# Half of one branch's attention weights transposed by VectorE in 32x32 blocks and through DRAM instead of by TensorE, in a two-layer hybrid encoder on one Trainium2 core

## The chip, the core and the metric

The kernel runs on one core of a Trainium2 chip (trn2). The metric is the device time of one execution in microseconds (us), lower is better. The inputs are those of `setup_inputs()`; weights are rearranged on the host before the launch and that is not in the time.

## What is computed

The reference is a trunk of two pre-norm residual layers over 512 tokens of width 1024, all in float32. In each layer the normalised input is projected by `w_in`, and the columns feed three token mixers of width 512: A, gated linear attention (4 heads, chunks of 64); B, differential softmax attention (4 heads, two score maps each); C, windowed attention with three dilations (8 heads of 64). Each is gated, projected back to 1024, merged with per-channel sigmoid gates and sent through `w_out`. The change is in mixer C:

```python
for window, dil in DIL_PATTERNS:                      # (128, 1), (512, 4), (2048, 16)
    o_g, lse_g = dilated_window_attention(qc, kc, vc, dil, window // (2 * dil))
    outs.append(o_g); lses.append(lse_g)
wts = jax.nn.softmax(jnp.stack(lses, axis=0), axis=0)
o_c = jnp.einsum('gbhs,gbhsd->bhsd', wts, jnp.stack(outs, axis=0).astype(f32))
y_c = o_c.transpose(0, 2, 1, 3).reshape(B, S, BRANCH_W).astype(x.dtype) * jax.nn.silu(c_g)
```

The three patterns together are one softmax over all 512 keys, with the logarithm of the number of patterns that hold a key (or a large negative number) added to the score. So the kernel needs, for each head of 64 and each block of 128 queries, a 128x512 tile of scores, its softmax, and the product of that with the values.

## The kernel before

**Groups.** A layer is worked in `NG` = 4 groups; group `i` holds head `i` of mixer A, head `i` of mixer B (two score maps) and heads `2i`, `2i+1` of mixer C. So there are 8 groups in all, and the first group of each layer has its own copy of the code (`first` is true), since the layer's norm is still being worked out; the other three run as a loop (`Fori`). After the four groups a layer has a branch stage (24 tiles `z`) and an output stage (8 tiles).

**Projections.** Each product with a weight tile is three float32r matmuls for each of 8 slices of the contraction: high and low parts of the activation (`hh`, `hl`) and of the weight (`wh`, `wl`). One slice is a *step* here, three matmuls of 128x512, and a tile has 8 steps. `product` at L1137 issues them. The two banks `proj` are used in turn; a product begins when the tile two before it has been read out of its bank (`bank_free`). A group's tiles in order are the values (four products of 384 columns, L1241), `a`, `bq`, `bk`, `cq`, `ck`, `ag`, `bg`, and then seven *fillers*: `cg`, `m0` to `m5`, 56 steps. `fill(n)` issues the next n of them. They stand between the attention's matmuls, so that TensorE has work while VectorE and ScalarE do the softmax.

**Weights.** SyncE (SP) loads each raw weight tile (512 KB) into one of 3 slots of `raw_w`, as soon as GpSimd (POOL) has split the one that was there. POOL splits it into `wh` (L424) and `wl` (L433, two halves), in one of 4 slots, as soon as TensorE has finished with the tile that was there. POOL also rotates mixer C's queries and keys (L471 to L475, L357). SP's queue holds, besides, the load of `up` for the next group.

**Attention.** 16 score tiles j = 0 to 15 are made by `scores(p)`, two at a time, into the banks `score0` and `score1`. Tiles 0 to 7 are mixer B's (four query blocks, two maps), 8 to 15 mixer C's. For each, VectorE (DVE) takes the row maximum (`row_max`: L958 for B; L964 for C, which also adds the mask and writes the negated scores to `sneg`), and ScalarE (ACT) the exponential with the row sum (`exp`, L721). 12 *units* u make the weights: units 0 to 3 are B's query blocks, from two tiles each, units 4 to 11 mixer C's, from tile j = u + 4 each. `weights(u)` on DVE takes the reciprocal of the sum (L1003) and scales the tile into `w` (L1005, for B L996 and L998). `turn_weights(u)` on TensorE (PE) transposes the four 128x128 blocks of `w` into a bank `turn` (L1302), and `turned(u)` on ACT copies the bank into `wt` or `wt1` (L729). At last `values` multiplies the transposed weights with the values (L1310): for B into `obank` after unit 3, for C into `mbank` at the end of the group, 16 matmuls of 64 output rows. DVE gates the result into `y` (L1038).

**Order on PE.** It is written out by hand. In numbers of steps: `scores(0)`, 4, `scores(1)`, 5, mixer A's outputs, unit 0, then for units 1 to 3 a pair of scores, 5 steps and the unit, then 3 steps, mixer B's values; then for units 4 to 9

```python
                    for u in range(4, 10):
                        if u % 2 == 0:
                            scores(u // 2 + 3)
                        fill(3 if u in (5, 7) else 4)
                        turn_weights(u)
```

then 4 steps, units 10 and 11, 3 steps and mixer C's values. `scores(p)` waits until the banks it overwrites were read. ACT's order has, besides the exponentials and copies, `tanh_gate` (for `cg`, which DVE then reads out of its bank, L941), `merge_gate(0)` to `merge_gate(5)` (L712: each reads one of `m0` to `m5` out of its bank, with a store to DRAM behind it), and the norms of A and B (L763 to L767, two activation table loads and three activations), after `merge_gate(2)`.

**End of the program.** The last output tile is worked in two halves of the tokens. `last_spread(h)` on PE (L1417) spreads a norm's factor into two banks, one for DVE (L1100) and one for ACT, POOL; both wait for both.

## Time and profile before

| | |
|---|---|
| median of 3 runs | 1237.7 us (1237.18 to 1238.46) |
| the profiled execution | 1239.5 us, of which its span is 1237.7 us |
| PE busy | 1215.9 us, 98% of the span |
| DVE busy | 700.7 us, 57% |
| ACT busy | 440.2 us, 36% |
| POOL busy | 832.3 us, 67% |
| DMA | 148.63 MB, 53136 packets |
| granted TensorE clock, mean | 0.995 |

A busy share is that of the whole span. A matmul's row gives its start and how long it was in the pipeline; the pace is the distance of the starts. PEld is the loading of weights into the array and overlaps PE. An idle time stands in brackets behind the instruction that ended it, with its releaser.

### The profile page before, as it was taken

What the parts mean: (1) busy time and instruction counts of PE and PEld (TensorE: products, weight loads), DVE (VectorE), ACT (ScalarE), POOL (GpSimd) and SP (SyncE); (2) the same over time, 40 slices, a digit from 0 to 9 for tenths busy, and PEclk for the clock granted to TensorE, in tenths of its full rate; (3) what the DMA queues carried; (4) which work ended last, traced back from release to release, by engine and by line L of the source; (5) the groups of instructions that cost most, each with busy time, mean ns of one, the idle gap of its engine ahead of it and who ended that gap; (6) DMA issues with size and microseconds to landing.
All of it is one profiled execution on the core that took longest, in us unless ns stands there. A gap on an engine that the chain in (4) does not pass through costs nothing.

```text
span 1237.7 us, 17755 instructions
## 1 busy us (share of the span) xinstructions
PE 1215.9 (98%) x5892; PEld 991.0 (80%) x5892; DVE 700.7 (57%) x1045; ACT 440.2 (36%) x800; POOL 832.3 (67%) x598
## 2 busy tenths in 40 slices
PE   7999999999999999999999999999999999999997
PEld 5877888788878887787888778887888788777886
DVE  6686227533753385677658841584257335648853
ACT  6425523542454235100253353245314532450011
POOL 5787377738762976677749753985398549857881
PEclk9999999999999999999999999999999999999998
DMA  6333233323332333374244222523252315336612
GB/s 240 102 108 124 96 102 106 111 94 108 104 104 93 119 102 124 126 259 154 90 155 143 87 97 81 159 79 110 73 165 85 120 51 153 102 102 223 218 69 69
DMA packets 53136, 148.63 MB, mean 120 GB/s; under 512 B 6880, under 2 KB 10464, under 8 KB 52704
## 3 DMA queue, kind: packets, MB, share of 16 engines
q1 hardware_dynamic: 30144, 103.04, 24.7%
q10 hardware_dynamic: 22944, 44.98, 11.8%
q8 instruction: 26, 0.43, 0.1%
q14 instruction: 22, 0.18, 0.0%
HBM read 114.45 MB, written 16.78 MB: 106 GB/s over the span
## 4 chain that ended last, share of the span: by engine, by line
PE 92%; DVE 4%; DMA 1%; issue 1%; ACT 1%; ACTq 0%; POOLq 0%; POOL 0%; DVEq 0%
PE proj L1137 52%; PE proj L1241 10%; PE turn L1376 4%; PE turn L1302 3%; PE score L1376 3%; PE score L1294 3%; PE score L1295 2%; PE mbank L1310 2%; PE obank L1310 2%; PE mbank L1376 2%; PE obank L1376 2%; PE proj L1155 1%; PE obank L1329 1%; DMA big<-big 1%; DVE yl L1048 1%
## 5 line engine op out<-in xcount | busy, mean ns | idle before, releaser
L433 POOL TENSOR_TENSOR wl<-raw_w,wh 128x512 fp32r<-128x512 f32 x352 | 505.1, 1455 | 31.7 <-POOL wh L424 31.7
L424 POOL TENSOR_SCALAR wh<-raw_w 128x1024 fp32r<-128x1024 f32 x176 | 213.6, 1214 | 287.3 <-issue 102.4
L1137 PE MATMUL proj<-hh,wh 128*128 128x512 f32 x1016 | 403.4, 397 | 0.5 <-DVE big L1075 0.5
L1137 PE MATMUL proj<-hh,wl 128*128 128x512 f32 x1016 | 398.2, 392 | 0.0
L1137 PE MATMUL proj<-hl,wh 128*128 128x512 f32 x1016 | 397.4, 391 | 0.0
L1137 PEld LDWEIGHTS proj<-hh,wh 128*128 128x128 f32 x1016 | 191.5, 188 | 40.7 <-issue 1.3
L1137 PEld LDWEIGHTS proj<-hh,wl 128*128 128x128 f32 x1016 | 191.1, 188 | 41.2
L1137 PEld LDWEIGHTS proj<-hl,wh 128*128 128x128 f32 x1016 | 191.5, 188 | 38.9
L544 ACT ACTIVATE six<-big 128x512 f32<-128x512 f32 x23 | 14.4, 626 | 198.1 <-DVE big L1075 198.1
L964 DVE CUSTOM_DVE_ANT_0 six<-score,lmask 128x512 f32<-128x512 f32 x64 | 43.2, 683 | 66.4 <-PE score L1295 66.4
L922 DVE TENSOR_TENSOR group<-big,group 128x512 f32<-128x512 f32 x24 | 37.6, 1617 | 71.7 <-ACT big L641 71.4
L729 ACT ACTIVATE big<-turn 128x512 f32<-128x512 f32 x96 | 56.1, 593 | 60.4 <-PE turn L1302 59.7
L721 ACT ACTIVATE six<-score,negmax 128x512 f32<-128x512 f32 x64 | 43.5, 684 | 82.4 <-DVE negmax L958 82.3
L1241 PE MATMUL proj<-wh,hh 128*128 128x384 f32 x192 | 64.9, 338 | 0.0
L1241 PE MATMUL proj<-wh,hl 128*128 128x384 f32 x192 | 64.3, 335 | 0.0
L1241 PE MATMUL proj<-wl,hh 128*128 128x384 f32 x192 | 64.2, 335 | 0.0
L1294 PE MATMUL score<-yh 128*128 128x512 f32 x128 | 57.0, 445 | 4.0 <-DVE group L953 3.8
L357 POOL TENSOR_TENSOR yh<-big,yh 64x1024 fp32r<-64x1024 f32 x16 | 38.4, 2399 | 32.4 <-ACT yh L664 30.9
L721 ACT ACTIVATE six<-six,negmax 128x512 f32<-128x512 f32 x64 | 45.9, 718 | 32.0 <-DVE negmax L964 32.0
L1302 PE MATMUL turn<-ident,w 128*128 128x128 f32 x384 | 56.3, 272 | 0.0
L1302 PEld LDWEIGHTS turn<-ident,w 128*128 128x128 f32 x384 | 46.6, 139 | 10.5
L624 ACT ACTIVATE big<-proj 128x512 f32<-128x512 f32 x32 | 19.2, 599 | 95.4 <-PE proj L1137 95.2
(239 smaller groups left out, 1923.4 us busy)
## 6 DMA issues: line engine op xcount, KB each, us to landing
raw_w<-weights SPq DMA_DIRECT2D x175, 512.0 KB, 3.3
gate_scratch<-gstage ACTq DMA_DIRECT2D x48, 256.0 KB, 2.1
six<-gate_scratch ACTq DMA_DIRECT2D x16, 768.0 KB, 5.1
big<-big ACTq DMA_DIRECT2D x64, 128.0 KB, 3.6
yh<-yh ACTq DMA_DIRECT2D x64, 128.0 KB, 2.4
big<-x_t SPq DMA_DIRECT2D x4, 512.0 KB, 6.4
big<-x_t SPq DMA_DIRECT2D x1, 2048.0 KB, 9.0
x_scratch<-big SPq DMA_DIRECT2D x1, 2048.0 KB, 7.3
```

The source lines that it names most:

```text
L357: return eng.tensor_tensor(yh[other, q_of(n, head):low_of(n, head) + 1:4, :], t[own, 0:2, :], yh[own, q_of(n, head):high_of(n, head) + 1:2 ...
L424: pool.tensor_scalar(wh[:, slot, :, :], src, 1.0, 1.0, ALU.mult, ALU.mult).then_inc(pool_high.sem, 1)
L433: ins = pool.tensor_tensor(wl[:, slot, half, :], src[:, half, :], wh[:, slot, half, :].bitcast(F32), ALU.subtract)
L721: act.activation(probs[:, j % 4, :], src, ACT.Exp, bias=negmax[:, j:j + 1], scale=k, accum_out=sums[:, j:j + 1]).then_inc(exp_done.sem, 1)
L729: act.activation((wt if u < 4 or u % 2 == 0 else wt1)[:, :, q:q + P], turn[u % 2][:, :].rearrange("p (k q) -> p k q", k=QB), ACT.Copy).the ...
L964: dve.tensor_tensor_reduce(sneg[:, j % 2, :], score[j % 2][:, :], lmask[:, S - P - P * b:2 * S - P - P * b], -1.0, 3.0e38, ALU.add, ALU.mi ...
L1137: last = pe.matmul(dst, a[:, slot, k, :], b[:, k, :], start=(k == 0 and a is wh and b is hh), stop=(k == KT - 1 and a is wl))
L1241: last = pe.matmul(proj[b % 2][:, 0:3 * P], a(k)[:, P * b:P * b + P], c[:, 0:3, k, :], start=(k == 0 and n == 0), stop=(k == KT - 1 and n ...
L1294: pe.matmul(score[head][:, :], yh[:, q_of(n, head), q], yh[:, high_of(n, head), :], start=True, stop=False)
L1302: last = pe.transpose(turn[u % 2][:, P * k:P * k + P], w[:, u % 2, P * k:P * k + P], ident[:, :])
L1310: last = pe.matmul(dst, v[:, k, cols], weights[:, k, :], start=(k == 0), stop=(k == QB - 1))
L1376: last = pe.matmul(zbanks[zt % 6][:, :], a[:, SLOT[c % BRANCH_SLOTS], n, :], (yl if is_low else yh)[:, b, :], start=(k == 0 and a is wh an ...
```

## The change

Units 4 to 9 (`VIA`) are no longer transposed by PE. For them:

- DVE only takes the reciprocal (`inverse`); ACT scales the tile in place in `probs` (`scale`); DVE transposes its 32x32 blocks (`turn_32`) into a buffer of two units (`pair_buffer`: `w` for the pairs 4, 5 and 8, 9, and two tiles of `group` for the pair 6, 7).
- SP sends each pair of units to DRAM with four DMAs, one for each 32 partitions, in runs of 256 bytes (`send`), and brings it back with four into `wt1` or `wt`, in runs of 1024 bytes (`bring`). The blocks are put in their places by the DRAM addresses.
- C's values wait for all three pairs (`back`).

Score tile j of mixer C is now query block j % 4 of head (j - 8) // 4, so that a pair is two neighbouring query blocks of one head. The tokens of the pairs come back interleaved by 32, and DVE undoes that as it gates `mbank` into `y`: four instructions of 64x128, two of 64x128 and one of 64x256 in the place of one of 128x512. Units 10 and 11 are scaled in `probs` and transposed by PE from there. The orders on PE, ACT, DVE and SP behind mixer B's values are written out anew: on ACT the norms of A and B stand ahead of `merge_gate(3)` and the last two exponentials. In a layer's first group 3 steps of the fillers stand ahead of `scores(0)` and 3 fewer at the end. At the end of the program `last_spread` signals each of its two banks by itself.

```diff
+VIA = list(range(4,10))
+BY_PE = [u for u in range(12) if u not in VIA]
+PAIRS = len(VIA) // 2
...
+        def by_quarter(t, n):
+
+            return t.rearrange("p n s -> p (n s)").rearrange("p (c k n j) -> p k c n j", c=4, k=QB, n=2)[:, :, :, n, :]
+
+        def pair_buffer(m):
+
+            return group[:, 8:10, :] if m == 1 else w
...
+        def w_free(G, u):
+
+            if u in VIA:
+                m = VIA.index(u) // 2
+                return sent[m - 2].at(G, 64) if m >= 2 else turn_done.at(G, len([n for n in BY_PE if n < u]))
+            return turn_done.at(G, BY_PE.index(u - 2) + 1)
...
+            def send(G, m):
+
+                sp.wait_ge(*turned_32.at(G, 2 * m + 2))
+                for a in range(4):
+                    sp.dma_start(turned_d[m, :, :, a, :], pair_buffer(m)[32 * a:32 * a + 32, :, :].rearrange("i n s -> i (n s)").rearrange(
+                        "i (x j) -> i x j", j=64)).then_inc(sent[m].sem, 16)
+
+            def bring(G, m):
+
+                u = VIA[2 * m]
+                if u == 4:
+                    sp.wait_ge(*c_parts.at(G, 1))
+                    apart(sp)
+                sp.wait_ge(*sent[m].at(G, 64))
+                if u == 8:
+                    sp.wait_ge(*out_done.at(G, 3))
+                    apart(sp)
+                k, q = (0 if u < 8 else QB), 2 * P * (u % 4 // 2)
+                for c in range(4):
+                    sp.dma_start(big[32 * c:32 * c + 32, k:k + QB, q:q + 2 * P], turned_d[m, :, QB * c:QB * c + QB, :, :].rearrange(
+                        "i x a j -> i x (a j)")).then_inc(back.sem, 16)
...
                         unit(L, i * GU + (4 + j), arrival(4 + j)[0])
+                        if j == 15:
+                            send(L * NG + i, 0)
+                    send(L * NG + i, 1)
+                    bring(L * NG + i, 0)
+                    send(L * NG + i, 2)
+                    bring(L * NG + i, 1)
+                    bring(L * NG + i, 2)
...
+                    def scale(u):
+
+                        j = 2 * u if u < 4 else u + 4
+                        act.wait_ge(*rs_ready.at(G, VIA.index(u) + 1))
+                        act.activation(probs[:, j % 4, :], probs[:, j % 4, :], ACT.Copy, scale=rs[:, j:j + 1]).then_inc(scaled.sem, 1)
...
-                act.wait_ge(*spread.at(h, 1))
+                act.wait_ge(*spread.at(h, 2))
...
+                    def inverse(u):
...
+                            j = u + 4
+                            dve.wait_ge(*exp_done.at(G, j + 1))
+                            dve.reciprocal(rs[:, j:j + 1], sums[:, j:j + 1]).then_inc(rs_ready.sem, 1)
+
+                    def turn_32(u):
+                        j = 2 * u if u < 4 else u + 4
+                        dve.wait_ge(*scaled.at(G, VIA.index(u) + 1))
...
+                        if u >= 2:
+                            dve.wait_ge(*w_free(G, u))
+                        dve.transpose(by_quarter(pair_buffer(VIA.index(u) // 2)[:, :, :], u % 2), probs[:, j % 4, :].rearrange("p (k c j) -> p k c j", k=QB, c=4)).then_inc(turned_32.sem, 1)
...
-                    dve.scalar_tensor_tensor(y[:, 2 * NG + i, :], mbank[:, :], 0.5, sg[:, 2, :], ALU.mult, ALU.mult).then_inc(y_read.sem, 1)
+                    h0, h1 = rows_of(0), rows_of(1)
+                    for b in range(QB):
+                        dve.scalar_tensor_tensor(tokens(y[h0, 2 * NG + i, :], b), by_token(mbank[h0, :], b), 0.5, tokens(sg[h0, 2, :], b), ALU.mult, ALU.mult)
+                    for b in range(2):
+                        dve.scalar_tensor_tensor(tokens(y[h1, 2 * NG + i, :], b), by_token(mbank[h1, :], b), 0.5, tokens(sg[h1, 2, :], b), ALU.mult, ALU.mult)
+                    t = slice(2 * P, 4 * P)
+                    dve.scalar_tensor_tensor(y[h1, 2 * NG + i, t], mbank[h1, t], 0.5, sg[h1, 2, t], ALU.mult, ALU.mult).then_inc(y_read.sem, 1)
...
+                    if first:
+                        fill(3)
                     scores(0)
...
+                    scores(5)
+                    fill(6)
+                    pe.wait_ge(*y_read.at(G, 2))
+                    mean_of(obank, 2)
+                    scores(6)
                     fill(4)
+                    scores(7)
+                    fill(13)
                     turn_weights(10)
+                    fill(2)
                     turn_weights(11)
-                    fill(3)
+                    fill(1 if first else 4)
                     assert filled == KT * len(FILLERS)
                     pe.wait_ge(*r_done.at(G, 1))
-                    values(12, out_done, (mbank[0:HD, :], slice(2 * P, 2 * P + HD), wt),
-                           (mbank[HD:P, :], slice(2 * P + HD, 3 * P), wt1))
+                    pe.wait_ge(*back.at(G, PAIRS * 64))
+                    pe.wait_ge(*wt_ready.at(G, len(BY_PE)))
+                    values(out_done, (mbank[0:HD, :], slice(2 * P, 2 * P + HD), wt1),
+                           (mbank[HD:P, :], slice(2 * P + HD, 3 * P), wt))
...
-                last.then_inc(spread.sem, 1)
+                    last.then_inc(spread.sem, 1)
```

**On DVE**, from the first row maximum of mixer C that follows mixer B's weights to the units that PE still transposes, before (ISA rows are the row maxima of L964, RECIPROCAL and TENSOR_SCALAR the weights):

```order
L1003 RECIPROCAL rs<-sums 128x1 [waits exp_done,turn_done]
L1005 TENSOR_SCALAR w<-six,rs 128x512 [waits dve_grp]
L964 ISA six,negmax<-score,lmask 128x512 [waits score_done,exp_done]
L964 ISA negmax 128x1
L1026 TENSOR_TENSOR yl<-group,yl 128x512 [waits sq_high_done,sq_done]
L1027 SCALAR_TENSOR_TENSOR y<-obank,sc,group 128x512
```

and with the change, to the third pair:

```order
L1098 RECIPROCAL rs<-sums 128x1 [waits exp_done] x2
L1045 ISA six,negmax<-score,lmask 128x512 [waits score_done,exp_done]
L1045 ISA negmax 128x1
L1110 STREAM_TRANSPOSE w<-six 128x4x4x32 [waits sent0,scaled]
L1045 ISA six,negmax<-score,lmask 128x512 [waits score_done,exp_done]
L1045 ISA negmax 128x1
L1110 STREAM_TRANSPOSE w<-six 128x4x4x32 [waits sent0,scaled]
L1151 TENSOR_TENSOR y<-y,group 128x512 [waits y_read,r_done]
L1152 TENSOR_TENSOR y<-y,group 128x512
L1084 RECIPROCAL rs<-sums 128x1 [waits exp_done]
L1086 TENSOR_SCALAR six<-six,rs 128x512 [waits dve_grp]
```

A unit of `VIA` is a reciprocal and a transpose on DVE now, with ACT's scaling between them; the last two transposes stand behind the row maxima of the last two tiles, and wait for the first pair's store (`sent0`).

**On SP**, from the last but one weight load of a group to the end of the group's body:

```order
L413 DMA raw_w<-weights 128x1024
L420 DMA turn_scratch<-w 512x1x64 [waits turned_32]
L420 DMA turn_scratch<-w 512x1x64 x3
L413 ISA [waits split_done]
L413 DMA raw_w<-weights 128x1024
L420 DMA turn_scratch<-group 512x1x64 [waits turned_32]
L420 DMA turn_scratch<-group 512x1x64 x3
L435 DMA big<-turn_scratch 32x4x256 [waits sent0]
L435 DMA big<-turn_scratch 32x4x256 x3
L420 DMA turn_scratch<-w 512x1x64 [waits turned_32]
L420 DMA turn_scratch<-w 512x1x64 x3
L435 DMA big<-turn_scratch 32x4x256 [waits sent1]
```

The last of a group's weight loads, and the loads of the next group behind them, now stand behind waits for DVE's transposes and for stores.

## Rows read from the trace of the kernel before

**Rows 1.** The page: busy time, granted clock and the chain that ended last.
```profile
PE 1215.9 (98%) x5892; PEld 991.0 (80%) x5892; DVE 700.7 (57%) x1045; ACT 440.2 (36%) x800; POOL 832.3 (67%) x598
...
PE 92%; DVE 4%; DMA 1%; issue 1%; ACT 1%; ACTq 0%; POOLq 0%; POOL 0%; DVEq 0%
```
**Rows 2.** Timeline of PE (start us, us), third group: turns and what stands around them.
```profile
356.48 0.39 PE L1295 MATMUL score<-yh 128*128 128x512 f32 x1
...
373.23 0.60 PE L1302 MATMUL turn<-ident,w 128*128 128x128 f32 x4
...
376.44 0.60 PE L1302 MATMUL turn<-ident,w 128*128 128x128 f32 x4
...
382.69 3.65 PE L1310 MATMUL mbank<-big,group 128*64 128x512 f32 x16
```
**Rows 3.** Timeline of PE, second group: first and last of 16 products, one slot each.
```profile
199.66 0.39 PE L1137 MATMUL proj<-hh,wl 128*128 128x512 f32 x1
...
203.29 0.39 PE L1294 MATMUL score<-yh 128*128 128x512 f32 x1
```
**Rows 4.** Timeline of PE, first groups of both layers: around the first scores.
```profile
82.59 0.47 PE L1294 MATMUL score<-yh 128*128 128x512 f32 x1 [1.98 <-DVE group L953]
...
94.70 0.40 PE L1137 MATMUL proj<-hh,wh 128*128 128x512 f32 x1
...
685.76 0.47 PE L1294 MATMUL score<-yh 128*128 128x512 f32 x1 [1.87 <-DVE group L953]
```
**Rows 5.** A window in layer 1's first group: busy times by engine, then granted clock.
```profile
684.00:692.00 8.00, 6.24 (x20) 5.00 (x21) 6.62 (x14) 2.08 (x5) 7.64 (x5) 0.79 0.00 0
```
**Rows 6.** Timeline of DVE: gate of `cg`; scalings and row maximum of mixer C.
```profile
98.18 0.67 DVE L941 SCALAR_TENSOR_TENSOR group<-group,proj 128x512 f32<-128x512 f32 x1
...
350.22 1.30 DVE L1005 TENSOR_SCALAR w<-six,rs 128x512 f32<-128x512 f32 x1
...
356.64 0.69 DVE L964 CUSTOM_DVE_ANT_0 six<-score,lmask 128x512 f32<-128x512 f32 x1 [5.12 <-PE score L1295]
...
358.96 0.49 DVE L1005 TENSOR_SCALAR w<-six,rs 128x512 f32<-128x512 f32 x1
```
**Rows 7.** Groups of DVE's instructions: count, busy us, mean ns.
```profile
L1038 DVE SCALAR_TENSOR_TENSOR y<-mbank,group 128x512 f32 x6 | 4.2, 692 | 52.6 <-PE mbank L1310 52.6
L982 DVE SCALAR_TENSOR_TENSOR state<-state,decay,turn 64x128 f32<-64x128 f32 x24 | 8.5, 353 | 0.3
```
**Rows 8.** Timeline of ACT, third group: an exponential, a merge gate, the norms.
```profile
357.37 0.73 ACT L721 ACTIVATE six<-six,negmax 128x512 f32<-128x512 f32 x1 [0.30 <-DVE negmax L964]
...
363.13 0.59 ACT L712 ACTIVATE gstage<-proj 128x512 f32<-128x512 f32 x1
364.26 1.28 ACT L763 ACT_TABLE_LOAD   x1 [0.54 <-ACT gstage L712]
...
368.13 1.06 ACT L767 ACTIVATE group<-group 128x1024 f32<-128x1024 f32 x1
```
**Rows 9.** Timeline of POOL, third group: the split of the last value tile.
```profile
376.11 1.04 POOL L424 TENSOR_SCALAR wh<-raw_w 128x1024 fp32r<-128x1024 f32 x1 [3.38 <-PE proj L1137]
```
**Rows 10.** DMA: share of 16 engines, 1231 to 1237.7 us; then issues, KB each, median us to landing.
```profile
q1 hardware_dynamic: 1383, 1.30, 57.3%
...
raw_w<-weights SPq DMA_DIRECT2D x175, 512.0 KB, 3.3
gate_scratch<-gstage ACTq DMA_DIRECT2D x48, 256.0 KB, 2.1
...
out_t<-y SPq DMA_DIRECT2D x4, 128.0 KB, 2.5
```
**Rows 11.** Timeline, end of layer 0's groups: DVE's low parts, PE's first low products.
```profile
508.03 6.11 DVE L1048 TENSOR_TENSOR yl<-y,yh 128x512 fp32r<-128x512 f32 x10 [0.21 <-DVE y L1038]
...
510.74 2.75 PE L1376 MATMUL score<-yl,wh 128*128 128x512 f32 x8
```
**Rows 12.** Timeline, end of the program: the spread of the first half's factor.
```profile
1225.83 0.61 PE L1417 MATMUL score<-ident,rcol 128*128 128x128 f32 x4
```

163 lines of the change are left out of this document (102 added, 61 removed).

## The prediction

> **What bounds the kernel now.** I read the page first. PE is busy for 98% of the span and carries 92% of the chain that ended last [rows 1]. So an instruction taken from PE is worth its slot, as long as nothing makes PE wait in its place; a busy share of 57% on DVE, 36% on ACT and 67% on POOL says that they have room on average, not that they are on time. Then I read PE's timeline. 16 products start in 3.63 us, 199.66 to 203.29 [rows 3]: one each 0.227 us, a step of three 0.68. Between the turns at 373.23 and 376.44 lie 3.21 us for one turn and 12 products [rows 2]; the products take 2.72, so a unit's turn costs 0.49 us, the slower start behind it included. PE waits inside the groups only twice, ahead of the first scores of each layer's first group, 1.98 and 1.87 us [rows 4]. The windows show what followed the second: over the 8 us from 684 on TensorE was granted 0.79 of its full clock on average [rows 5], that is 3.4 us at its lower level, 1.2 in the place of 2.4 GHz, which cost 1.7 us of matmul time. Behind the first wait, of about the same length, it kept the full level.
>
> **What goes.** 6 turns in each of 8 groups at 0.49: 48 x 0.49 = -23.4 us. ACT copied each of them out of its bank and now scales each tile instead, which is the same work; DVE's scaling becomes a transpose.
>
> **The first groups' fill.** 3 steps (2.04 us) ahead of the first scores fill the waits of 1.98 and 1.87 us [rows 4]: -3.85. But 3 steps more are done at every later place, and a product must find its bank read. `m1` is step 16. Before, it began three steps into the fill behind unit 1; now it begins behind the fourth step of the one behind unit 0. That fill starts at 94.70 [rows 4], four steps later it is 97.4, and `m1` takes the bank of `cg`, which DVE reads from 98.18 for 0.67 us [rows 6]: free at about 98.9. PE waits 1.5 us, in both first groups: +3.0. `m5` comes later, below.
>
> **A group behind mixer B's values.** I lay the new order over the third group's trace. The last matmul of `scores(5)` starts at 356.48 [rows 2], so PE goes on at 356.7: 6 steps to 360.8; the mean's two matmuls to 361.3; `scores(6)`, four slots, to 362.2; 4 steps, 364.9; `scores(7)`, 365.8; 13 steps, 374.7; unit 10, 2 steps, unit 11, 4 steps: C's values could start at 379.8, against 382.69 before [rows 2].
>
> DVE and ACT: a row maximum takes 0.69 [rows 6], an exponential 0.73 and 0.18 more for its sum [rows 8]. ACT's scaling has no row; a merge gate's activation of the same 128x512 takes 0.59 [rows 8], so 0.6. The transpose has no row either. Its bounds are the two durations of the scaling that it replaces, 0.49 alone and 1.30 when a POOL instruction ran at the same time [rows 6]; I take 0.65, nearest to the row maxima, which like it are one pass over a 128x512 tile. The Trainium skill ("SBUF — State Buffer", Who interferes with whom) says that a DVE instruction with at most one SBUF input outside the two-port modes doesn't contend with GpSimd. By that the transposes stay near the low end while POOL splits weights; were they held up as the scalings are, each would be at the upper one.
>
> With these, tile 10's maximum ends at 357.3, the transpose of unit 4 (behind ACT's squares) at 358.5, tile 11's maximum at 360.9, in time for `scores(6)` at 361.3. Maxima 12 and 13 end at 363.3, transposes 6 and 7 at 365.5; ACT ends scaling 9 at 366.9; the maxima of 14 and 15, with transposes 8 and 9 between and behind them, end at 368.7. ACT then does the norms, 4.9 us from table load to end [rows 8], to 371.9, `merge_gate(3)` to 372.5 and its store's issue to 372.9, exponential 14 to 373.8. DVE scales unit 10 from 374.0. There POOL is at work: the split of the last value tile starts when `m4` is done, at 376.11 before [rows 9], at 373.4 now. So the scaling takes up to 1.3 and not 0.49, and PE, there at 374.7, waits about 0.4 us: +0.4 in each of the 6 other groups, +2.4 (bounds 0 and 0.9 each). In a first group `m5` (step 48) is due at 371.3 by the same count, but its bank is `m3`'s, read by `merge_gate(3)` at 372.5: +1.1 in each, +2.2, and the wait at unit 10 is hidden.
>
> **The way through DRAM.** 1383 packets took 57.3% of 16 engines in 6.7 us [rows 10]: 44 ns each, nearly all of 1024 bytes. For a packet of 256 bytes I have no row: not above 44, and, at a quarter of the bytes, not below 11. I take 16 ns, nearer to the low end, since stores of twice the bytes, 256 KB and 128 KB, land in about the same time [rows 10] and so little of it goes by packets. A pair is 2048 packets, 128 on each engine: 2.0 us (1.4 to 5.6) beside the issues of four DMAs, and another 2.1 us, a store's time to land [rows 10], behind the last issue at the most. The third pair starts at 368.9, when SP has the two transposes, and has landed by 373. The way back is 512 packets of 1 KB, 1.4 us of data beside four issues, and 2.5 for 128 KB to land [rows 10]: by 377. C's values are ready to start at 380.1. That hides it with 3 us to spare, 2 in a first group. Cost 0. The first pair's store (361.5 to 365.5) frees `w` for transpose 8 at 366.7, also in time.
>
> SP's queue: the last value tile's load stands behind the first pair, which goes out at 361.5, and is wanted at 373.4; it takes 3.3 us [rows 10]. The next group's `up` and `a` go out behind the third pair's return, at about 375; `up` is wanted at 382, `a`'s split after 380. Nothing there.
>
> **The gate of `mbank`.** One instruction of 0.69 us becomes seven. 64x128 with two tensors takes 0.35 [rows 7]; six at 0.3 and one of 64x256 at 0.4 are 2.2: 1.5 us more. Inside a layer it is covered by the next group's first value product, 4 us. At a layer's end it is not: DVE's low parts start at 508.03, right behind the gate, and PE's 8 products with them take 2.75 us where 1.8 is their pace [rows 11]. PE already waits for DVE there, so the 1.5 us come through, in both layers: +3.0 (bounds +2.3 and +3.8, with the seven at 0.25 to 0.35 and 0.35 to 0.5).
>
> **The end.** DVE no longer waits for the second bank of the spread, which PE starts at 1225.83 [rows 12] and gives away nearly 0.4 us later; the last update follows on it: -0.35. In the second half POOL and ACT still wait for both.
>
> **Sum.** -23.4 - 3.85 + 3.0 + 2.4 + 2.2 + 3.0 - 0.35 = -17.0. The clock's fall in layer 1 I leave in: the wait before it goes, one of 1.5 us comes a little later. The profiled execution took 1239.5 us, its span is 1237.7, and so is the median of the runs: profiled I expect 1222.5, as a median **1220.7**.
>
> **Rivals.** *The added waits don't come* (DVE and ACT a little quicker than I laid them out): -23.4 - 3.85 + 3.0 - 0.35 and 1.7 less for 3.4 us at half clock: 1211.4. For it: every one of these waits is under 1.6 us. Against: a bank's reader is in a fixed order, and `cg`'s gate has its row. Chance 0.10.
>
> *The softmax chain is late.* Transposes at their upper bound, 1.30, put 3.9 us more on DVE by unit 10, of which about 2 reach PE in each group, since exponential 14 waits behind the norms anyway: 8 x 2 = 16 us back, 1236. At half of that, 1229. For it: the two ways from exponential to scaling to transpose cross between ACT and DVE at each unit. Chance 0.24 for 1226 to 1237.
>
> *The third pair is late, and the kernel slower.* Place: PE's last wait of a group, for `back`. All pairs go through one queue. With p ns for a packet of 256 bytes, the second pair's data starts at 365.6 and takes 0.128 p; the first pair's return, 1.4, and the third pair's data, 0.128 p, stand behind it; 1.2 to land and 3.6 for the return: 371.8 + 0.256 p. At 16 ns my time stands; at 32 ns it is 380.0, just in time; at 40 ns 382.1, 2 us late in 8 groups, and the gain is gone; at 44 ns, the row's price for 1 KB, 383.1: 3 us, +24, and if the clock falls behind each such wait as in rows 5, 1.7 more each, +13.6: 1245 to 1258. The Trainium skill ("DMA: Bandwidth & Descriptors", Specifications) says that transfers under 512 bytes make the engine read, modify and write. As a mechanism here that is a packet at twice its time or more, 32 ns and up; it would be at the edge of my slack or past it. No row shows such stores. Chance 0.12 for slower, and 0.04 more that it ends within 0.2%.
>
> *The orders don't do what they say*, for instance a weight load late behind SP's waits, so that POOL and PE start a group late: the slack is 7 us there, so I give it no chance of its own.
>
> **Numbers.** My forecast, 1215 to 1226, has 0.50; the rivals as above. The range leaves out the slow end and the lower half of the first rival: 1213 to 1236. Faster by over 0.2% (which is about what a measurement of this kernel can tell from no change, 2.5 us) 0.84, within it 0.04, slower 0.12.
>
> **What would show it.** PE's turns 192 in the place of 384; no wait ahead of the first scores; waits of PE at L1261 (a filler for its bank) of 1.5 and 1.1 us in two groups; one of about 0.4 at unit 10; none at C's values. Transposes near 0.65 us. The low products at a layer's end over 3.5 us. A wait at the values' line in all 8 groups, with DMA as releaser, would make this wrong, and so would transposes of over 1.2 us.

## The result, and the profile after

| | before | changed |
|---|---|---|
| median | 1238.1 us (4 runs, 1237.2 to 1239.0) | 1262.7 us (4 runs, 1261.7 to 1265.2) |
| ratio | | 1.0205, 95% interval 1.0193 to 1.0217 |
| profiled execution, span | 1239.5, 1237.7 us | 1262.2, 1260.1 us |
| mean granted clock | 0.995 | 0.986 |

The change makes the kernel 2% slower. The forecast, 1220.7, was on the wrong side; the rival that ended on this side (the third pair late, 1245 to 1258) named the place, and even its upper end is 5 us short.

The page of the changed kernel, to be held against [rows 1]: PE is busy for 6.4 us less, but has lost its hold on the chain, in which SyncE's queue and the DMAs now stand.

```profile
PE 1209.5 (96%) x5700; PEld 973.2 (77%) x5700; DVE 708.7 (56%) x1093; ACT 445.5 (35%) x800; POOL 830.7 (66%) x598
...
PE 81%; SPq 7%; DMA 4%; DVE 4%; issue 2%; ACT 1%; DVEq 0%; POOLq 0%; POOL 0%; ACTq 0%
```

PE's waits (engine, line, waited for: us in total, times, longest us):

```profile
PE mbank L1435 <- DMA big<-turn_scratch: 27.0, 8, 3.9
...
PE proj L1261 <- DVE group L1022: 2.8, 2, 1.4
PE proj L1261 <- ACT gstage L782: 2.2, 2, 1.1
PE turn L1428 <- DVE six L1086: 1.8, 8, 0.2
```

The first line is new and is 27 us: C's values (L1435) wait for the pairs in all 8 groups. The next three are the waits that I had priced. The waits ahead of the first scores [rows 4] are gone.

The third group on PE, where [rows 2] shows what stood there before, and then two windows (us, PE, PEld, DVE, ACT, POOL busy, granted clock, DMA share, GB/s):

```profile
389.03 6.63 PE L1435 MATMUL mbank<-big,group 128*64 128x512 f32 x16 [3.49 <-DMA big<-turn_scratch]
```
```profile
384.00:388.00 4.00, 1.54 (x7) 0.94 (x5) 0.00 (x0) 0.60 (x1) 0.00 (x0) 1.00 1.03 255
388.00:396.00 8.00, 6.97 (x18) 2.17 (x19) 0.15 (x1) 0.31 (x1) 3.53 (x3) 0.57 0.58 221
```

The values take 6.63 us where they took 3.65: after the wait of 3.49 us the clock was 0.57 of full on average over 8 us, which is 6.9 us at its lower level, 3.4 us lost. That is the worst of the eight groups: in the other seven, behind waits of 2.85 to 3.87 us, the values take 5.1 to 5.4 us. Over the whole execution the mean of 0.986 is 35 us at that level.

SyncE's queue in the same group, a row for each run of DMA issues:

```profile
366.50 3.37 SPq L420 DMA_DIRECT2D turn_scratch<-w  x4
370.14 0.44 SPq L413 DMA_DIRECT2D raw_w<-weights  x1
370.81 2.93 SPq L420 DMA_DIRECT2D turn_scratch<-group  x4
373.95 2.73 SPq L435 DMA_DIRECT2D big<-turn_scratch  x4
376.80 3.40 SPq L420 DMA_DIRECT2D turn_scratch<-w  x4
380.24 4.64 SPq L435 DMA_DIRECT2D big<-turn_scratch  x8
```

and the end of the chain of waits there, single issues:

```profile
373.95 1.30 SPq L435
...
378.76 1.44 SPq L420
...
384.43 4.48 DMA big<-turn_scratch
```

SyncE issues 20 DMAs from 370.81 on without a pause. Most take 0.43 (loads) or 0.6 us (stores), some 0.8 to 1.4. The third pair's transposes end at 374.1,

```profile
373.41 0.70 DVE L1110 STREAM_TRANSPOSE w<-six 128x512 f32<-128x512 f32 x1
```

but its stores begin at 376.80, behind the first pair's loads; the last load is issued at 384.4 and lands 4.5 us later (a landing is counted from the start of its issue). One of the third pair's transposes had itself waited, for the first pair's store to free `w`:

```profile
372.19 0.71 DVE L1110 STREAM_TRANSPOSE w<-six 128x512 f32<-128x512 f32 x1 [0.43 <-DMA turn_scratch<-w]
```

For landings of stores SyncE itself waits once, for 0.7 us in the whole execution:

```profile
SPq L431 <- DMA turn_scratch<-w: 0.7, 1, 0.7
```

All the while the DMA engines are close to full, where they had been half empty before (here 372 to 376 us of the changed kernel, then of the kernel before):

```profile
372.00:376.00 4.00, 4.00 (x19) 3.34 (x18) 1.93 (x4) 3.95 (x5) 2.35 (x3) 1.00 0.90 245
```
```profile
372.00:376.00 4.00, 4.00 (x22) 3.26 (x21) 3.62 (x10) 2.29 (x6) 0.73 (x1) 1.00 0.59 197
```

### The profile page after: what moved, and what is told of

Read it like the earlier page. It is cut to its first block, busy times and chain, and to the rows that moved or that the text cites. A ratio compares the mean times of both kernels' runs of the same rounds, so it can differ in the third digit from the quotient of the medians.

```text
span 1260.1 us, 17507 instructions
## 1 busy us (share of the span) xinstructions
PE 1209.5 (96%) x5700; PEld 973.2 (77%) x5700; DVE 708.7 (56%) x1093; ACT 445.5 (35%) x800; POOL 830.7 (66%) x598
## 4 chain that ended last, share of the span: by engine, by line
PE 81%; SPq 7%; DMA 4%; DVE 4%; issue 2%; ACT 1%; DVEq 0%; POOLq 0%; POOL 0%; ACTq 0%
PE proj L1261 44%; PE proj L1365 9%; PE turn L1506 4%; SPq L420 3%; PE mbank L1435 3%; SPq L435 3%; PE score L1506 3%; DMA big<-turn_scratch 3%; PE obank L1435 2%; PE score L1418 2%; PE score L1419 2%; PE mbank L1506 2%; PE obank L1506 2%; DMA turn_scratch<-w 1%; PE proj L1279 1%
## 5 line engine op out<-in xcount | busy, mean ns | idle before, releaser
L1435 PE MATMUL mbank<-big,group 128*64 128x512 f32 x128 | 43.3, 839 | 27.0 <-DMA big<-turn_scratch 27.0
L1158 DVE SCALAR_TENSOR_TENSOR y<-mbank,group 64x128 f32 (+1 forms) x32 | 7.1, 276 | 99.9 <-PE mbank L1435 99.9
L1435 PEld LDWEIGHTS mbank<-big,group 128*64 128x64 f32 x128 | 12.7, 191 | 53.7 <-issue 53.7
```

The costliest lines, as they stand in the source:

```text
L1435: last = pe.matmul(dst, v[:, k, cols], weights[:, k, :], start=(k == 0), stop=(k == QB - 1))
```

## The experiments

All times are medians; the ratio is to the kernel before, run on the same chip. "Start of values" is the time from the start of `scores(5)` to that of C's values in the third group (changed kernel: 360.52 and 389.03). It and the waits are those of the profiled execution, which is not the median one: 1243.7 us in run 4, 1265.0 in run 9 and 1234.8 in run 12.

| | median us | ratio, 95% interval | PE's waits at values, us | start of values |
|---|---|---|---|---|
| changed kernel | 1262.7 | 1.0205 (1.0193 to 1.0217) | 27.0 | 28.5 |
| 1 no way back | 1221.4 | 0.9857 (0.984 to 0.9873) | none | 25.0 |
| 2 stores first | 1260.4 | 1.0182 (1.0161 to 1.0204) | 23.1 | 27.6 |
| 3 PE kept busy | 1248.2 | 1.0084 (1.0062 to 1.0106) | 3.1 | 28.2 |
| 4 short runs back | 1240.7 | 1.0009 (0.9996 to 1.0021) | 15.8 | 26.2 |
| 5 heads apart | 1248.3 | 1.0076 (1.0061 to 1.0091) | 5.7 and more | 26.3 |
| 6 all three mends | 1237.5 | 0.9997 (0.9987 to 1.0008) | none | 25.0 |
| 7 two pairs | 1222.9 | 0.9872 (0.9858 to 0.9887) | none | 25.4 |
| 8 gates not stored | 1246.3 | 1.0068 (1.0044 to 1.0093) | 21.8 | 26.0 |
| 9 few bytes | 1259.3 | 1.0154 (1.0138 to 1.017) | 28.2 | 28.2 |
| 10 two pairs, 2 steps ahead | **1219.3** | 0.9845 (0.9832 to 0.9859) | none | |
| 11 two pairs, 0 steps ahead | 1223.3 | 0.9873 (0.9858 to 0.9888) | none | |
| 12 second queue | 1239.3 | 1.0006 (0.9989 to 1.0022) | 12.4 | 25.6 |

### 1. Without the way back

```diff
                     send(L * NG + i, 1)
-                    bring(L * NG + i, 0)
                     send(L * NG + i, 2)
-                    bring(L * NG + i, 1)
-                    bring(L * NG + i, 2)
...
-                    pe.wait_ge(*back.at(G, PAIRS * 64))
+                    for m in range(PAIRS):
+                        pe.wait_ge(*sent[m].at(G, 64))
```

> The changed kernel with the four loads of each pair left out; TensorE waits for the three pairs' stores instead, so the products of units 4 to 9 with the values work on what the buffer held before, and the output is not the reference's. Theory A (the way through DRAM is the whole miss: SyncE issues 24 DMAs a group one behind the other, so the third pair comes late, and each wait is followed by 3.4 us at half clock): the stores have landed at about 383.5 of the third group, TensorE is ready at 385.5, so the wait at the values goes and the falls of the clock with it: 1262.7 - 27 - 15 = about 1221, 1218 to 1225. Theory B (the rest of the sum is off as well: transposes and scalings, or the short stores disturbing other work): over 1228.

1221.4. Everything but the way through DRAM came out as the sum had it, to 0.7 us. The values' row of the third group has no wait and its old 3.65 us:

```profile
376.28 3.65 PE L1432 MATMUL mbank<-big,group 128*64 128x512 f32 x16
```

So the whole miss, 41 us, is at one wait.

### 2. Stores ahead of loads

```diff
                     send(L * NG + i, 1)
-                    bring(L * NG + i, 0)
                     send(L * NG + i, 2)
+                    bring(L * NG + i, 0)
```

> Only the order on SyncE's queue is changed: the second and the third pair's stores go out ahead of all loads. Same DMAs, same bytes. Theory A (order and issue time on SyncE's queue): the third pair's first store is issued when its transposes are there, at about 374.1 in the third group where it was 376.8; the last load lands at about 387.3 instead of 389.0, TensorE is ready at 385.5 and waits 1.8 instead of 3.5 us: 8 x 1.7 = 13 us less, 1249, and 1236 if the clock's falls go with it. Theory B (the data itself, stores of 256-byte packets, fills the time): no change, 1260 to 1265.

1260.4, 2 us less, hardly clear of the scatter, and not 13 to 26. The third pair's stores do start earlier, as expected; but the loads then stand in one block, and end only 1.1 us earlier than in the changed kernel, counted from `scores(5)` (359.55 here):

```profile
373.18 3.09 SPq L420 DMA_DIRECT2D turn_scratch<-w  x4
376.48 6.37 SPq L435 DMA_DIRECT2D big<-turn_scratch  x12
```

My theory that the order on the queue is the fault falls. An order can't shorten 20 issues in a row.

### 3. TensorE kept busy in the wait

```diff
                     pe.wait_ge(*r_done.at(G, 1))
+                    pe.wait_ge(*wt_ready.at(G, len(BY_PE)))
+                    for _ in range(12):
+                        pe.matmul(turn[0][:, :], mean[:, :], hh[:, 0, :], start=True, stop=True)
                     pe.wait_ge(*back.at(G, PAIRS * 64))
```

> Twelve matmuls of 128x512 without use are put on TensorE between its last filler of a group and its wait for the pairs, 2.7 us of work inside a wait of 3.4; nothing else changes. Theory C (of the miss of 42 us some 14 are the clock, which falls behind each idle wait): with a wait of under 1 us the falls go, 1262.7 - 14 = about 1249. If the falls have another cause: 1262, not under 1260. If the matmuls outlast the wait in the first groups, some 1 to 3 us are added in both cases.

1248.2: 14.5 us come back though the pairs are as late as before. The rows: work, a wait of 0.40, the values at their full pace, and full clock behind them.

```profile
382.94 2.97 PE L1485 MATMUL turn<-hh,mean 128*128 128x512 f32 x12
386.31 3.65 PE L1435 MATMUL mbank<-big,group 128*64 128x512 f32 x16 [0.40 <-DMA big<-turn_scratch]
```
```profile
386.00:394.00 8.00, 7.69 (x40) 5.17 (x41) 2.02 (x8) 0.31 (x1) 3.58 (x3) 1.00 0.57 215
```

With a mean clock of 0.997 against 0.986, 28 us fewer at half speed, 14 us by the clock alone. So the 41 us are 27.0 of waiting and 14 of what the clock does behind it.

### 4. Runs of 1024 bytes out and 256 back

```diff
-                    sp.dma_start(turned_d[m, :, :, a, :], pair_buffer(m)[32 * a:32 * a + 32, ...
-                        "i (x j) -> i x j", j=64))
+                    sp.dma_start(turned_d[m, a, :, :, :].rearrange("c i x -> i c x"), pair_buffer(m)[32 * a:32 * a + 32, ...
+                        "i (c x) -> i c x", c=4))
...
-                    sp.dma_start(big[32 * c:32 * c + 32, k:k + QB, q:q + 2 * P], turned_d[m, :, QB * c:QB * c + QB, :, :] ...
+                    sp.dma_start(big[:, k:k + QB, q + 64 * c:q + 64 * c + 64], turned_d[m, c, :, :, :] ...
...
-    turn_scratch = nc.dram_tensor("turn_scratch", (PAIRS, 32, 16, 4, 64), F32, kind="Internal").ap()
+    turn_scratch = nc.dram_tensor("turn_scratch", (PAIRS, 4, 4, 32, 4 * 64), F32, kind="Internal").ap()
```

> The DRAM buffer is laid out so that the stores go in runs of 1024 bytes and the loads in runs of 256; the number of DMAs, their order and bytes stay. Theory A (issue and landing, not packets, set the time): within 3 us of 1262.7. Theory B (a store of 256 bytes costs the engine a second pass, a load doesn't): the last landing comes 1 us or more earlier, 8 us or more faster, under 1255.

1240.7: 22 us less for the same bytes in the same number of packets and DMAs. It isn't the packets' time: a packet of 256 bytes took 19 ns on average in the changed kernel and 18 here, and the time of the pairs' packets in that group, as a share of 16 engines, is about equal (13.1 and 12.7 us). What became shorter is the stores' issue and their landing. Issues of the changed kernel, then of this one (KB each, median us from issue to landing):

```profile
big<-turn_scratch SPq DMA_DIRECT2D x96, 128.0 KB, 3.3
...
turn_scratch<-w SPq DMA_DIRECT2D x64, 128.0 KB, 3.7
turn_scratch<-group SPq DMA_DIRECT2D x32, 128.0 KB, 3.9
```
```profile
big<-turn_scratch SPq DMA_DIRECT2D x96, 128.0 KB, 3.2
...
turn_scratch<-w SPq DMA_DIRECT2D x64, 128.0 KB, 2.7
turn_scratch<-group SPq DMA_DIRECT2D x32, 128.0 KB, 3.0
```

Stores in long runs land 0.9 to 1.0 us sooner; loads in short runs no later. The issue of a store takes 0.44 us where it was 0.64, that of a load 0.63 where it was 0.43 (medians). Which of the two did it this run can't tell. SyncE can issue the third pair's loads when it is through with the second pair's and the third pair's stores have landed. Counted from the start of `scores(5)` in the third group, the one ends at 22.3 and the other at 22.1 us in the changed kernel, at 20.3 and 19.8 here: two ways of nearly the same length, and both became shorter. The last load is issued 1.5 us earlier (22.4 for 23.9) and lands 3.65 us behind its issue where it was 4.48. That DVE no longer waits for the first pair's store gains nothing: the third pair's transposes end at 13.1 for 13.6, but its stores begin at 15.2 and 16.3, when the queue comes to them.

Between the profiled executions, 18.5 us apart, 11.2 are waits. The rest is the clock, 0.991 for 0.986, some 6.5 us: it did not fall behind each wait any more. Two of the eight groups:

```profile
746.95 6.27 PE L1434 MATMUL mbank<-big,group 128*64 128x512 f32 x16 [3.83 <-DMA big<-turn_scratch]
869.80 3.65 PE L1434 MATMUL mbank<-big,group 128*64 128x512 f32 x16 [1.84 <-DMA big<-turn_scratch]
```

### 5. The two heads' products apart

```diff
-                        for k in range(QB):
-                            for dst, cols, weights in products:
+                        for dst, cols, weights in products:
+                            if dst is products[-1][0] and len(products) == 2:
+                                pe.wait_ge(*back[1].at(G, 64))
+                                pe.wait_ge(*wt_ready.at(G, len(BY_PE)))
+                            for k in range(QB):
...
-                    pe.wait_ge(*back.at(G, PAIRS * 64))
+                    pe.wait_ge(*back[0].at(G, 128))
```

> The products with the values are done head by head, not alternating: the first head's eight wait only for the first two pairs, the second head's eight for the third. Nothing else changes. In the third group TensorE is ready at 385.5 and the last load lands at 388.9; the second pair's loads land some 2 us before. So the first head's 1.8 us of products stand inside the wait: 8 x 1.8 = 14 us less, 1248, and down to 1236 if a wait of about 1 us isn't followed by the clock's fall. If the first two pairs come hardly earlier than the third (all DMAs served side by side), no more than 4 us: 1258 to 1262.

1248.3, the number expected, but not by the way expected. The values start 2.2 us earlier than in the changed kernel, with the first head, and the wait is short enough that the clock stays at 1.00 behind it. But the products themselves became slower, as run 6 shows without any wait: 1.8 us in each group. 27.0 - 5.7 - 8 x 0.8 (the second head's wait: this kernel's row takes 6.20 and that of run 6 5.42) = 15 of waiting and 14 of clock are gained, 8 x 1.8 = 14 given back: 1248.

### 6. Short runs back, stores first and heads apart, together

```diff
                     send(L * NG + i, 1)
-                    bring(L * NG + i, 0)
                     send(L * NG + i, 2)
+                    bring(L * NG + i, 0)
...
-                            for dst, cols, weights in products:
+                        for dst, cols, weights in products:
```

on the runs of experiment 4.

> Runs of 1024 bytes out and 256 back, the third pair's stores ahead of the loads, and the heads' products apart. By the run with short runs back, where TensorE was ready at 381.2 and the last load landed at 382.2 of the third group: the first head is in time, the second head's products start at 383.0 and find it there. No wait at the values, no clock fall: 1221, 1219 to 1225, below both kernels. If the stores put first delay the first head's loads past 381.2: 1225 to 1235.

1237.5, the kernel before within its uncertainty, where I expected 1221. There is indeed no wait, and the clock is 0.997. What is left is in the values' row, and in the loads of their weights, inside each block one every 0.43 us (where the blocks meet, two or three, as in the last line):

```profile
379.68 5.42 PE L1437 MATMUL mbank<-big,group 128*64 128x512 f32 x16
380.16 0.14 PEld L1437 LDWEIGHTS mbank<-big,group 128*64 128x64 f32 x1 [0.29 <-issue]
380.59 0.14 PEld L1437 LDWEIGHTS mbank<-big,group 128*64 128x64 f32 x1 [0.29 <-issue]
...
381.44 0.19 PEld L1437 LDWEIGHTS mbank<-big,group 128*64 128x64 f32 x3 [0.29 <-issue]
```

In run 1, where the heads alternate, two of them stand in the same time:

```profile
376.76 0.14 PEld L1432 LDWEIGHTS mbank<-big,group 128*64 128x64 f32 x2 [0.28 <-issue]
377.19 0.14 PEld L1432 LDWEIGHTS mbank<-big,group 128*64 128x64 f32 x2 [0.28 <-issue]
```

5.42 - 3.65 = 1.77 us in 8 groups is 14.2: 1221.4 + 14.2 = 1235.6; the profiled execution took 1236.1.

### 7. Two pairs only

```diff
-VIA = list(range(4,10))
+VIA = list(range(4,8))
...
-                    fill(13)
+                    fill(7)
+                    turn_weights(8)
+                    fill(2)
+                    turn_weights(9)
+                    fill(4)
                     turn_weights(10)
```

Units 8 and 9 get `weights` on DVE and `turned` on ACT again, and DVE's gate of `mbank` is five instructions.

> Only units 4 to 7 go through DRAM, in two pairs; units 8 and 9 are scaled by VectorE and turned by TensorE again. 16 DMAs a group on SyncE's queue in the place of 24. 1220.7 from my own sum, plus 16 turns of 0.49 us = 1228.5, if two pairs are in time (in the third group they would be back at about 381, TensorE comes at 386): 1226 to 1232. If two pairs are late as well: over 1238.

1222.9, better than both kernels and 5.6 under my sum. The loads are issued by 368.3 and there is nothing to wait for:

```profile
363.42 4.89 SPq L435 DMA_DIRECT2D big<-turn_scratch  x8
```
```profile
375.50 3.65 PE L1429 MATMUL mbank<-big,group 128*64 128x512 f32 x16
```

The waits at unit 10 (1.8 us) and for `m3`'s bank (2.2) are gone too, since PE comes to both later; that is 4 of the 5.6.

### 8. The gates' stores left out

```diff
-                        act.dma_start(gate_d[i * 6 + m, :, :], gstage[:, m % 2, :])
+                        if first and L == 0:
+                            act.dma_start(gate_d.rearrange("(g n) p s -> n p g s", n=6)[m], gstage[:, m % 2:m % 2 + 1, :].to_broadcast([P, NG, S]))
+                        else:
+                            act.dma_start(gate_d[i * 6 + m, :, 0:4], gstage[:, m % 2, 0:4])
```

> Beside the three pairs, ScalarE's queue sends the merge gates of 256 KB to DRAM, three of them in that stretch. Here the very first group writes all four groups' gates once and the others store 4 columns instead of 512, so the output is not the reference's. SyncE's queue is as it was. If the DMA engines' own time is what makes the pairs late (they are busy for 0.8 to 1.0 from 368 to 388 of the third group, the three gate stores 2.9 us of it): the last load lands 1.5 to 3 us earlier, 12 to 24 us less and the clock's falls with it, 1225 to 1245. If it is SyncE's issuing alone: no change, 1259 to 1265.

1246.3, just above the range for the engines' own time. SyncE's queue has the same DMAs in the same order, and yet the values start 2.5 us earlier in the third group: the last load is issued 1.4 us earlier and lands in 3.4 us for 4.5. In the first group, which stores four times as much, the wait grew from 2.85 to 12.3 us:

```profile
151.47 6.60 PE L1438 MATMUL mbank<-big,group 128*64 128x512 f32 x16 [12.30 <-DMA big<-turn_scratch]
```

The other seven wait 9.5 us together, 1.4 each for 3.4. Other transfers on the engines, even from another engine's queue, move this wait both ways.

### 9. A sixteenth of the bytes

```diff
-                        "i (x j) -> i x j", j=64)).then_inc(sent[m].sem, 16)
+                        "i (x j) -> i x j", j=64)[:, :, 0:4]).then_inc(sent[m].sem, 16)
...
-                    sp.dma_start(big[32 * c:32 * c + 32, k:k + QB, q:q + 2 * P], ...
+                    sp.dma_start(big[32 * c:32 * c + 32, k:k + QB, q:q + 16], ...
...
-    turn_scratch = nc.dram_tensor("turn_scratch", (PAIRS, 32, 16, 4, 64), F32, kind="Internal").ap()
+    turn_scratch = nc.dram_tensor("turn_scratch", (PAIRS, 32, 16, 4, 4), F32, kind="Internal").ap()
```

> The changed kernel with the same 24 DMAs a group in the same order and with the same number of pieces, but pieces of 16 bytes out (256 before) and 64 back (1024 before), so one sixteenth of the data; most of what is multiplied with the values is what the buffer held, and the output is not the reference's. If the time on the DMA engines holds the pairs up and SyncE's issuing only backs up behind it: the wait at the values goes, 1221 (1219 to 1225), and the issues take 0.43 to 0.64 us with none over 1. If issuing itself is the limit (by its pieces, not its bytes): 20 issues still take 12 us or more from the second pair's transposes, the last load lands less than 1.5 us earlier than in the changed kernel, 1240 to 1263.

1259.3. The numbers are those of the second expectation (20 issues in 16 us, the last load landed 0.4 us earlier), but not for its reason. The DMA engines were only a third to two thirds busy, and no issue on that group's chain took over 1.11 us; but the wait stayed at 28.2 us. SyncE now stood still for landings of stores, in all 8 groups, and the chain shows them:

```profile
SPq L431 <- DMA turn_scratch<-w: 24.4, 8, 4.2
```
```profile
367.11 6.14 DMA turn_scratch<-w
...
373.26 1.11 SPq L435
...
377.90 5.73 DMA turn_scratch<-w
```

A store of 8 KB in pieces of 16 bytes lands 6 us behind its issue, longer than 128 KB in pieces of 256 did. A packet of 16 bytes took 9 ns, so this isn't the packets' time on the engines. The median from issue to landing over the kernel goes with the size of the pieces: 2.7 and 3.0 us at 1024 bytes (run 4), 3.7 and 3.9 at 256, 4.6 and 5.8 here.

```profile
turn_scratch<-w SPq DMA_DIRECT2D x64, 8.0 KB, 4.6
turn_scratch<-group SPq DMA_DIRECT2D x32, 8.0 KB, 5.8
```

As a test of issuing against bytes the run was badly chosen: it took bytes away and lengthened the landing.

### 10 and 11. Two or no steps ahead of the first scores

```diff
                     if first:
-                        fill(3)
+                        fill(2)
                     scores(0)
...
-                    fill(1 if first else 4)
+                    fill(2 if first else 4)
```

> Two pairs through DRAM, and 2 steps instead of 3 ahead of a layer's first scores, 1 more at that group's end. The first step of m1 then stands behind the next pair of scores, where cg's bank has been read: its wait of 1.4 us goes in both layers (-2.8); ahead of the first scores 0.68 us less is covered, of which 0.6 and 0.5 come back as waits (+1.1). 1222.9 - 1.7 = 1221.2. If the bank's wait only moves: 1223 to 1224.

> Two pairs through DRAM, and the 3 steps ahead of a layer's first scores put back to the group's end, as in the kernel before. By my terms: the waits of 1.98 and 1.87 return (+3.85), those for cg's bank go (-2.8), and the clock's fall in layer 1 may return (+1.7): 1222.9 + 1.1 to 2.8 = 1224.0 to 1225.7. If the fill ahead brought nothing: 1222.9 within 0.5.

1219.3 with 2 steps and 1223.3 with none, beside 1222.9 with 3. Run 10 is 1.9 us better than expected: the 1.1 us of waits that I had coming back ahead of the first scores did not come (no wait over 0.2 us is left there). Filling 3 steps ahead brought nothing that can be measured: the waits of 1.4 us for `cg`'s bank cost what the fill gains. With 2 steps neither wait is left; PE's waits over 0.5 us in run 10 are all outside the groups. Without the fill 1.9 us of waiting are back ahead of the first scores in the first layer (full clock behind it, 1.00 from 82 to 90 us). In the second layer there is none at that place, but there are two a little later, 0.71 at unit 0 and 0.99 at a pair of scores. With these 3.6 for my 3.85, and 2.8 off for `cg`'s bank, it would be 1223.7; the other 0.4 is within the runs' scatter (1222.5 to 1225.2).

```profile
82.01 0.47 PE L1412 MATMUL score<-yh 128*128 128x512 f32 x1 [1.90 <-DVE group L1032]
```

### 12. The third pair's loads from ScalarE's queue

On top of run 4, with the stores first:

```diff
                     exp(15)
+                    act.wait_ge(*sent[2].at(G, 64))
+                    for c in range(4):
+                        act.dma_start(big[:, QB:2 * QB, 64 * c:64 * c + 64], turned_d[2, c, :, :, :]...).then_inc(back.sem, 16)
                     turned(10)
```

> Three pairs, runs of 1024 bytes out and 256 back, all stores ahead of the loads on SyncE's queue, and the third pair's four loads issued from ScalarE's queue, behind the last exponential. TensorE is ready for the values 25.0 us after it begins scores(5); with the short runs back the loads were there 26.1 after it. If SyncE's one queue is the limit: the third pair's store has landed at 17.6, ScalarE is free at 19.3 and issues until 21.8, landed at 25.3: waits of 0.3 us, 1221.4 + 2.4 = about 1224 (1221 to 1228). If the landing of the loads grows by what the second queue brings forward: 1236 to 1241, as with the short runs back.

1239.3, as the second expectation had it: no better than run 4, whose interval it shares. The last issue begins 20.1 us behind the start of `scores(5)` (352.75 here), 2.3 earlier than in run 4; but the last load takes 5.30 us to land, where it took 3.65, with the DMA engines full (second row below). The Trainium skill ("DMA: Bandwidth & Descriptors", Rules for kernel authors) says that DMAs spread over more issuing engines gain no bandwidth, since all run on the same 16, and save only the time of issuing. With 2.3 us saved at issuing the trace agrees; that the landing takes 1.7 us longer stands in this trace, not in the rule.

```profile
372.88 5.30 DMA big<-turn_scratch
```
```profile
372.00:376.00 4.00, 3.77 (x21) 2.96 (x20) 1.90 (x3) 1.77 (x4) 2.90 (x3) 1.00 1.25 246
```

## Why the prediction was wrong

Run 1 says that every term of the sum but one held: 1221.4 for 1220.7. (The sum's first term, 48 x 0.49, is 23.5 and not 23.4.) The step that failed is "The third pair starts at 368.9 ... has landed by 373 ... by 377 ... That hides it with 3 us to spare ... Cost 0". Counted from the start of `scores(5)` (355.38 in the trace that I had laid it over; 356.48 is its last matmul), I had the third pair's stores start at 13.5 us, the last load back at 21.6 and PE ready at 24.7. Measured: 16.3, 28.4 and 25.0. The 6.8 us by which the way is longer are

- 0.1: the third pair's transposes end at 13.6, nearly as counted. Within that, "frees `w` for transpose 8 ..., also in time" failed as well: the first pair's store landed at 11.6 and not 10.1, and the transpose waited 0.43 us for it;
- 2.7: its stores then stand in SyncE's queue behind the first pair's four loads. I had priced each pair's way as if it were alone, and looked at the queue only for what stands behind the pairs;
- 2.0: from the first of these stores to the last load's issue 7.6 us for 5.6. An issue takes 0.43 or 0.6 us and more when the engines are full; 12 of them follow one another here;
- 2.0: the last load lands in 4.5 us, not 2.5. I had taken 2.5 from `out_t` [rows 10], four DMAs at the end of the program, where no other queue sends data.

3.1 of it were to spare and PE came 0.3 later than counted: 3.4, for the 3.49 of the trace. The clock did the rest, as the rival had foreseen from [rows 5]; I had it at 1.7 us a group and it averages 1.8.

**The price of a packet** was not the fault: 19 ns for my 16, against 11 to 44. The rival's sum (3 us late at 44 ns) came to the right wait by a wrong cause. The Trainium skill ("DMA: Bandwidth & Descriptors", Specifications) says that transfers under 512 bytes make the engine read, modify and write. The packets' time on the engines shows no doubling: medians of 18 ns for 256 bytes, 28 for 516 and 46 for 1024 in the changed kernel. But the landing of the stores, 3.8 against 2.9 us, and 5 us for 16 bytes, does show that short pieces cost in a store to DRAM and not in a load from it. Whether that is the rule's mechanism no run here can tell. The same page of the Trainium skill (Anatomy of one DMA, on DMAs that GpSimd issues) puts most of a DMA's fixed time, about 2 us, on the wait until the last byte is confirmed in the target memory, longest for DRAM. The stores here are issued by SyncE, and those of run 9, of 8 KB, took 4.6 to 5.8 us with hardly any time on the engines; what that time is made of no run shows.

**What of the lateness is issuing, engine time or landing** isn't one of them alone. In the changed kernel the queue and the landing of the third pair's stores let the third pair's loads go at nearly the same time (22.3 and 22.1 us in the third group), so that shortening one of them alone could gain little there. Runs 2 and 12 changed the issuing (1.1 and, against run 4, 2.3 us earlier) and got 0.9 and 0.6 at the values. Run 8 took transfers off the engines and got 2.5. Run 4 changed the pieces, and with them issues and landings, and got 2.3. My first theory, SyncE's issuing, explains 20 issues in a row but not run 12. Open is how much of the landing at 256 bytes is the pieces' own and how much the full engines': in run 8 the same stores land in 3.0 and 3.3 us where it was 3.7 and 3.9. What is settled is that no order tried brought three pairs back within 25 us, and that two fit (run 7). Run 4's pieces with the stores first, and the heads still alternating, were not tried on one queue.

The other terms, by their rows:

| term | predicted | measured |
|---|---|---|
| `m1` waits for `cg`'s bank | 1.5 us twice | 1.4 twice |
| `m5` waits for `m3`'s bank | 1.1 twice | 1.1 twice |
| unit 10 | 0.4 in 6 groups | 0.2 in 8 |
| first scores | no wait left | none left |
| transpose, scaling | 0.65, 0.6 us | 0.71, 0.72 us |
| `mbank`'s gate | 1.5 us more | 1.1 more: 1.80 for 0.69 |
| low products at a layer's end | 1.5 us more | 1.1 more |
| the end | 0.35 less | DVE's first update starts 0.45 sooner behind the spread |

The gate and the products behind it in run 1, for [rows 11]:

```profile
498.36 0.88 DVE L1155 SCALAR_TENSOR_TENSOR y<-mbank,group 64x128 f32 x4 [7.60 <-PE mbank L1432]
499.25 0.50 DVE L1157 SCALAR_TENSOR_TENSOR y<-mbank,group 64x128 f32 x2
499.67 0.42 DVE L1159 SCALAR_TENSOR_TENSOR y<-mbank,group 64x256 f32 x1
```
```profile
501.96 3.81 PE L1504 MATMUL score<-yl,wh 128*128 128x512 f32 x8
```

All 48 transposes took 704 to 714 ns, though half of them stand beside one of POOL's splits, where scalings had been held up to 1.30 us [rows 6]. The Trainium skill ("SBUF — State Buffer", Who interferes with whom) says that a DVE instruction with at most one SBUF input, outside the two-port modes, doesn't contend with GpSimd; the trace agrees.

## What to carry to other kernels

Work that is taken off the bottleneck and sent through DRAM must be priced as a queue: all its DMAs in order, each with its issue, on engines shared with everything else in that stretch, and with a landing time read from a busy stretch, not from a quiet one. Here the last third of the work was worth 1.5 us at best (1221.4 against 1222.9, and the intervals of the two overlap) and cost 40 when it came 2.9 to 3.9 us late: 27 of waiting, and the rest mostly clock, which fell behind each such wait. Leave the last, latest portion on the bottleneck engine, and store in long pieces even if the loads then are in short ones.

## What I hadn't expected of the hardware

- **Products with 64 output rows run two at a time** if they alternate between the two halves of the output partitions: 3.65 us for 16 alternating, 5.42 in two blocks, with the same operands (runs 1 and 6). Products of 128 rows with the same type go one every 0.43 us (8 of mixer B's in 3.43). The Trainium skill ("TensorE: Matmul & The Clock Gate", Part 3: Packing small matmuls) says that matmuls that use different tiles of the array run at the same time; the trace agrees for the two column halves. The old order of the loops had this, and nothing in the code says so.
- **A store's landing depends on its pieces more than on its bytes**: 2.7 to 3.0 us for 128 KB in pieces of 1024 bytes, 3.7 to 3.9 in pieces of 256 (3.0 to 3.3 with other transfers away, run 8), 4.6 to 5.8 for 8 KB in pieces of 16. Loads in pieces of 256 bytes landed in 3.2 us, those in pieces of 1024 in 3.3.
- **An issue's time goes with the number of pieces**: 0.62 to 0.64 us (medians) for 512 of them, of 256 or of 16 bytes, out or back; 0.43 to 0.44 for 128, of 1024 or of 64 bytes (changed kernel, runs 4 and 9).
- **A short wait leaves the clock alone.** Of the waits at C's values in the changed kernel and in runs 2, 3, 4, 5, 8, 9 and 12, all 26 of 2.4 us and more were followed by a fall of the granted clock, and none of the 34 of up to 2.2 us was; of two between them, 2.34 us in run 2 was and 2.36 in run 12 wasn't. Elsewhere in the program it is less clear: of the waits of 1.9 us ahead of the first scores one was followed by a fall [rows 4, 5], the other and that of run 11 weren't.
